# One instruction instead of two for the low part of each weight tile, in a two-block model in float32

## What is computed

```
for i in range(DEPTH):
    ...
    h = rmsnorm(x, g[2])
    f = jnp.square(jax.nn.relu(h @ mlp_w1[i])) @ mlp_w2[i]
    x = x + rmsnorm(f, g[3])
```

## Time and profile before

| | before |
|---|---|
| median of three runs | 2306.93 us (2304.56 to 2310.94) |
| profiled execution | 2310.81 us |
| its span | 2309.0 us |
| granted TensorE clock, mean | 0.996 of full speed |
| PE busy | 2272.0 us, 98% |
| DVE busy | 1717.7 us, 74%, 2043 instructions |
| ACT busy | 1318.4 us, 57%, 1769 instructions |
| DMA | 513.26 MB, mean 222 GB/s |

### The profile page before, as it was taken

How to read it: one execution, slowest core, us unless ns; L and a number is a source line. 1 busy time by engine, 2 the same in 40 slices (tenths; PEclk the granted TensorE clock), 3 DMA queues, 4 the chain that set the end, 5 groups by cost and what they waited for, 6 DMA issues and landing times.

```text
span 2309.0 us, 26586 instructions
## 1 busy us (share of the span) xinstructions
PE 2272.0 (98%) x10609; PEld 1873.5 (81%) x10609; DVE 1717.7 (74%) x2043; ACT 1318.4 (57%) x1769; POOL 81.1 (4%) x110
## 2 busy tenths in 40 slices
PE   9999999999999999999999999999999999999998
PEld 7778788878788888888887888888888888888887
DVE  6575864888788788887879788878878775456664
ACT  6444444766665655656666656656656564444453
POOL 0000000000000000000000000000000010000000
PEclk9999999999999999999999999999999999999999
DMA  9445455777787787787575886786786745653343
GB/s 342 158 162 182 163 183 183 273 215 256 243 259 250 252 243 246 242 252 274 218 279 159 277 272 192 279 275 187 274 284 189 265 160 197 253 186 147 146 151 123
DMA packets 73100, 513.26 MB, mean 222 GB/s; under 512 B 8234, under 2 KB 8565, under 8 KB 13520
## 3 DMA queue, kind: packets, MB, share of 16 engines
q1 hardware_dynamic: 61568, 429.58, 49.1%
q0 software_dynamic: 11264, 81.87, 15.9%
q10 hardware_dynamic: 144, 0.12, 0.0%
HBM read 505.24 MB, written 6.29 MB: 222 GB/s over the span
## 4 chain that ended last, share of the span: by engine, by line
PE 82%; DVE 10%; DMA 3%; ACT 2%; issue 1%; POOL 0%; ACTq 0%; POOLq 0%; DVEq 0%
PE P L353 80%; DVE low L616 6%; DMA raw<-in_w_d 3%; PE P L356 3%; ACT hi L497 1%; DVE R_m L601 1%; DVE X L601 1%; DVE EV L601 1%; DVE R_f L601 0%; DVE R_f_r L601 0%; DVE X L604 0%; ACT EV L553 0%; DVE R_h L604 0%; DVE R_g_r L601 0%; DVE st L604 0%
## 5 line engine op out<-in xcount | busy, mean ns | idle before, releaser
L616 DVE TENSOR_TENSOR low<-raw,hi 128x1024 fp32r<-128x1024 f32 (+3 forms) x694 | 810.2, 1200 | 409.1 <-ACT hi L497 406.5
L497 ACT ACTIVATE hi<-raw 128x1024 fp32r<-128x1024 f32 (+3 forms) x694 | 701.7, 1040 | 473.9 <-PE P L353 332.4
L353 PE MATMUL P<-hi,R_h 128*128 128x512 f32 (+2 forms) x2944 | 950.9, 395 | 13.6 <-DVE EV L601 10.7
L353 PE MATMUL P<-hi,R_f_r 128*128 128x512 f32 x2480 | 792.8, 392 | 5.3 <-DVE R_m L601 3.5
L353 PEld LDWEIGHTS P<-hi,R_h 128*128 128x128 f32 x2944 | 553.9, 188 | 135.4 <-issue 22.5
L353 PE MATMUL P<-low,R_h 128*128 128x512 f32 (+2 forms) x1472 | 571.3, 388 | 0.0
L353 PEld LDWEIGHTS P<-hi,R_f_r 128*128 128x128 f32 x2480 | 465.8, 188 | 107.4 <-DVE low L616 7.7
L353 PE MATMUL P<-low,R_f_r 128*128 128x512 f32 x1240 | 482.9, 389 | 0.0
L353 PEld LDWEIGHTS P<-low,R_h 128*128 128x128 f32 x1472 | 277.8, 189 | 56.2 <-issue 4.6
L616 DVE TENSOR_TENSOR low<-R_f,hi 128x1024 fp32r<-128x1024 f32 x226 | 261.9, 1219 | 31.3 <-ACT hi L497 31.3
L353 PEld LDWEIGHTS P<-low,R_f_r 128*128 128x128 f32 x1240 | 233.1, 188 | 46.5
(11 more groups left out here) (221 smaller groups left out, 1458.8 us busy)
## 6 DMA issues: line engine op xcount, KB each, us to landing
raw<-in_w_d SPq DMA_DIRECT2D x128, 1024.0 KB, 7.4
raw<-in_w_u SPq DMA_DIRECT2D x72, 1024.0 KB, 5.7
R_f<-in_w_u POOLq DMA_DIRECT2D x56, 1024.0 KB, 9.2
raw<-in_w_z SPq DMA_DIRECT2D x45, 1024.0 KB, 4.9
raw<-in_w_i SPq DMA_DIRECT2D x36, 1024.0 KB, 4.8
R_f<-in_w_u SPq DMA_DIRECT2D x28, 1024.0 KB, 9.3
X<-in_w_u SPq DMA_DIRECT2D x28, 1024.0 KB, 12.8
raw<-in_w_mo SPq DMA_DIRECT2D x16, 1024.0 KB, 4.8
```

What stands on the lines that cost most here:

```text
L353: return self.e.matmul(o, l, r, start=start, stop=stop, skip_group_check=True)
L497: self.e.activation(hi, raw, ACT.Copy).then_inc(*self.inc("high_made", ("high", k, d)))
L616: self.e.tensor_tensor(low, raw, hi.bitcast(f32), ALU.subtract).then_inc(*self.inc("low_made", *lows))
```

## The change

The high parts are made as before, in two pieces with a semaphore for each. For every tile that is split in two, the low part is now made by one instruction over the whole tile (`split_low`), which waits for the second high piece and then makes all four low blocks known at once. Tiles split in four pieces stay as they are. Nothing else is altered.

```
--- before.py
+++ after.py
@@ -343,7 +343,7 @@
         gated_silu = gated_v = gates = half_dft = half_silu = halved_rstd = halves = head_columns = inverse = load_piece = load_tile = \
         masked_exp = memory_out = mla_out = nsa_out = ones_row = plain_exp = plain_parts = padded_keys = pool_scale = pool_windows = \
         product = norm_mean = norm_part = norm_whole = norm_root = relu_square = residual = rope = rope_keys = scale = scaled_parts = scores = side_load = side_taps = sine = sine_of = \
-        split = square_sum = store = tile_sum = chain_load = chain_add = combine = operand_sum = times_row = times_row_apart = pads = group_sums = tail_keys = tail_rows = turn = v_times_k = values = warm = y_back = idle
+        split = square_sum = store = tile_sum = split_low = split_high = chain_load = chain_add = combine = operand_sum = times_row = times_row_apart = pads = group_sums = tail_keys = tail_rows = turn = v_times_k = values = warm = y_back = idle
 
 
 class Pe(Engine):
@@ -491,6 +491,11 @@
     def copy(self, o, i, done, **scale):
         self.e.activation(o, i, ACT.Copy, **scale).then_inc(*self.inc("act_done", done))
 
+    def split_high(self, k, d, hi, raw, ready, free):
+        self.wait_ge(ready)
+        self.wait_ge(free)
+        self.e.activation(hi, raw, ACT.Copy).then_inc(*self.inc("high_made", ("high", k, d)))
+
     def split(self, k, d, hi, raw, low, ready, free, *lows):
         self.wait_ge(ready)
         self.wait_ge(free)
@@ -614,6 +619,10 @@
     def split(self, k, d, hi, raw, low, ready, free, *lows):
         self.wait_ge(("high", k, d))
         self.e.tensor_tensor(low, raw, hi.bitcast(f32), ALU.subtract).then_inc(*self.inc("low_made", *lows))
+
+    def split_low(self, k, hi, raw, low):
+        self.wait_ge(("high", k, 1))
+        self.e.tensor_tensor(low, raw, hi.bitcast(f32), ALU.subtract).then_inc(*self.inc("low_made", *[("low", k, q) for q in range(4)]))
 
     def cols_ready(self, m):
         self.wait_ge(m)
@@ -1087,7 +1096,12 @@
         free = None
         if o >= NO:
             free = "used", user[o - NO], 2 * d // n if plan[user[o - NO]][3] == c else 1
-        E.split(k, d, m.hi[o % NO][0:parts, q], raw[0:parts, q], m.low[o % NO][0:parts, q], ready, free, *lows)
+        if n == 2:
+            E.split_high(k, d, m.hi[o % NO][0:parts, q], raw[0:parts, q], ready, free)
+            if d == 1:
+                E.split_low(k, m.hi[o % NO][0:parts, 0:c], raw[0:parts, 0:c], m.low[o % NO][0:parts, 0:c])
+        else:
+            E.split(k, d, m.hi[o % NO][0:parts, q], raw[0:parts, q], m.low[o % NO][0:parts, q], ready, free, *lows)
         if d == n - 1:
             user[o] = k
             if kind == "chain":
```

## The result

| | before | after |
|---|---|---|
| median | 2308.18 us (2304.56 to 2310.94, 4 runs) | 2384.48 us (2381.91 to 2386.93, 4 runs) |
| ratio, 95% interval | | 1.033 (1.0318 to 1.0343) |
| profiled execution, its span | 2310.81, 2309.0 us | 2382.13, 2380.3 us |
| granted TensorE clock, mean | 0.996 | 0.990 |

The kernel is 3.3% slower, 76 us. The forecast was 36 to 37 us slower, 2344, with a range up to 2372. The direction was right. The size was half of what came, and the time lies outside the range, at the upper end of the third rival.

What follows compares the result with a forecast made beforehand. The prediction took TensorE's matmuls as the bound, with 23.4 us of PE waits for DVE as the ceiling of gain. Terms -2 + 18 + 12 + 6 + 3 = +37 us gave 2344 us, range 2312 to 2372.

Steps and rivals of the forecast that it cites:

- the third rival: Late low parts free raw's buffer later, so loads and next parts slip further: 63 us or more, 2370 to 2385; 10%.
- What is removed: 478 instruction pairs become single ones, saving 38 us of DVE time, nearly all beside PE's work; counted as -2 us.
- The first kind of place: Down tile after half-length up tiles: DVE starts only on the second high piece, PE late; 13 x 1.4 = 18 us.
- the three rows behind the 1.4: Three worked steps at the down tile after half-length up tiles: PE 2.0, 1.4 and 1.0 us late; middle taken.
- The thirteen places: Down tiles after half-length up tiles found short of slack, one of fourteen steps having enough; 1.4 us each.
- The second kind: Combine in EV, queued on DVE behind the waiting low part: PE's wait 0.9 to about 1.9 us; 12 us in all.
- The third kind: Low part and sums into R_m some 17 us later, queued behind a merged tile: 14 x 0.4 = 6 us.
- The fourth kind: Starts of both MLPs and the first mixer, where DVE is behind: PE waits for the whole tile; together 3 us.
- The lateness is covered: Rival: after PE's first loss, loads and ACT's work have slack, later places not late; up to 7 us, 2311; 9%.
- DVE's shorter work wins: Rival: DVE reaches MLP tiles late with both high pieces ready, so shorter work cuts PE's waits; faster, 2295; 5%.
- the lateness feeds itself: Rival: raw's buffer is freed up to 1.07 us later, delaying loads and next parts; 4.5 us a step, 2370 to 2385; 10%.

Runs made afterwards that it cites:

- two pairs of edits: Changed kernel, fourth and fifth down tiles in two pieces: 1.0213, 1.025, both 1.0205; kernel before, sums and sixth combine moved ahead of splits: 1.0017, 1.0001, both 0.9952.

## Why the prediction was wrong in size

*What is removed* held. A merged tile takes 2290 ns, DVE lost 38 us, and none of it is seen in the time.

*The first kind of place* was found right and priced too low. The step is the bound on a late load: "the load itself comes 0.5 us later because its buffer was freed later", with 0.5 as the upper end and nothing of it in the value taken. PE's start of the fourth down tile against the third moved from 10.94 to 12.79 us, 1.85 a step and 26 us over fourteen, where 18 were taken. Its load landed 0.8 us later against PE in the mean. In the third step PE's start moved by 3.4 us: the 2.0 of the working, and nearly all the rest by a high part that came 1.5 us later against PE. In the second step it moved by 1.3 where 1.4 was worked out. The late part came not through the freed buffer, as the step had it, but with the adds.

One of the three rows behind the 1.4 was read wrongly. The product at 1796.76 us is that of the sixth down tile of the last step, not the fourth, and PE waited there only 0.2 us in all fourteen steps. The fourth is here:

```profile
1770.25 2.01 ACT L497 ACTIVATE hi<-raw 128x1024 fp32r<-128x1024 f32 x2 [5.55 <-DMA raw<-in_w_d]
...
1773.83 0.39 PE L353 MATMUL P<-hi,R_f_r 128*128 128x512 f32 x1
```

The same working gives 1770.25 + 2.01 + 2.53 = 1774.79, 1.0 us late, and PE came 1.1 late. That the wrong row gave the same value was luck. The thirteen places "short of slack" were all fourteen: PE waited at least 0.48 us at each.

*The second kind* held to a tenth. The wait is 1.82 us ("about 1.9"), and PE loses 0.93 us in twelve of the steps, 13 us in all, where 12 were taken.

*The third kind* was 6 us and its sum came out: waits for R_m rose by 4.9 us, and PE's start there moved by 6.0 in all. The reason given was half right. The queue behind a merged down tile plays its part, but the run with up tiles alone shows the same place at 13.3 us by merged up tiles. Why it is smaller with the change no run shows; I think that PE had waited before.

*The fourth kind* was 3 us with 4 as its upper bound. With the half-clock time taken off, PE loses 2.0 us ahead of the first MLP, most of it at the start of the first mixer, and 1.0 and 1.7 us over the starts of the two MLPs, 4.7 in all. Another 5 us came between the MLPs and behind them, which the prediction let go as nothing.

*The term that was missing* is the clock. The prediction counted a microsecond of PE's wait as a microsecond and said: "PE's busy time stays at about 2272 us, and the span grows by its waits." It was 2295.6 us. The longer waits also brought the half clock: 28.7 us more of it, 14 us of time in the profiled execution and about 20 in the mean of the four. The two runs with filled waits show that the waits are its cause. From the starts of all products in both traces, with half of the half-clock time taken off, the 71 us by which the span grew are 26.2 + 12.7 + 6.0 for the first three kinds, 4.7 for the starts, 5.0 outside the MLPs, 3.1 in small pieces of the steps and 13.6 of clock.

*The rivals.* "The lateness is covered" is out: it was not. "DVE's shorter work wins" is out as well. The trace agrees with the Trainium skill's page "Perfetto Trace Analysis", section "Optimizing Scalar/DVE Operations": DVE was busy 74% of the span and held PE up, and there breaking up instructions was the better form. The advice to minimize the number of operations in the Trainium skill's page "VectorE: DVE Perf Modes", section "Rules for kernel authors", which the page gives for chained DVE operations, was no guide here: with 478 operations fewer the kernel is 3.3% slower. The rival that came nearest in time was "the lateness feeds itself", 2370 to 2385 at 10%. Its loads do land late, by 0.8 us in the mean at the fourth down tile, but not because the buffer is freed late: with the third down tile in two the buffer came earlier and the load did not. What it lacked is the adds, and it too had no clock in it. That the measured time lies in this rival's interval is therefore partly luck. The range was too narrow at its upper end because a known chain (low part, add, load, high part) was given 0.5 us by judgement, and because no row was read for what a longer wait does to the clock, although the windows of the profile have the column.

## What to carry to other kernels

An instruction that is merged over two inputs waits for the later one, and so does everything behind it in its queue; price it at the consumers that were released just in time, which no list of waits shows (the fourth down tile had 0.1 us of waits before and 24.2 after), and not by the busy time saved. Follow a late completion through every transfer that it releases, count the waits of TensorE with what they do to its clock, and when one wait is removed look for the place that waits next: here two pairs of edits did not add up, one giving less and one more than its parts. Before comparing two variants, take the clock out of both times.

## What I had not expected of the hardware

PE waits of 1.8 to 3.9 us in an otherwise full stream were enough to bring the clock to 1.2 GHz behind them, in some steps and not in others with the same wait: of the twelve EV waits of 1.82 us six were followed by it. The twelve EV waits of 0.89 us in the kernel before were followed by none. Filling the waits with 13 useless matmuls a step made the kernel 14 us faster.

Adding DMAs carried half of what plain loads carried at the same share of the engines, in these two stretches of the kernel before, columns as in the earlier trace rows:

```profile
676.00:680.00 4.00, 4.00 (x20) 3.30 (x19) 4.00 (x5) 1.81 (x2) 0.00 (x0) 1.00 1.00 201
688.00:692.00 4.00, 4.00 (x19) 3.31 (x18) 2.48 (x3) 3.58 (x4) 0.00 (x0) 1.00 1.01 426
```

The first has only GpSimd's adds under way and moves 201 GB/s at a share of 1.00, the second only SyncE's plain loads and moves 426 GB/s at 1.01. Whether it is the adding or the other queue that costs this, no run separates. Behind two such adds a load that was issued 0.8 us earlier did not land earlier.
